# One decoder layer on one core: a later wait for the post-norm row, moved low parts and squares, and GpSimd making sums of weight blocks

## The chip, the cores and the metric

The kernel runs on one core of a Trainium2 chip. The metric is device time in microseconds of one execution, the median of several runs. The engines are called by the profile's names: PE (TensorE, matmuls), PEld (its weight loads), DVE (VectorE), ACT (ScalarE), POOL (GpSimd), SP (the queue that issues most transfers).

## The reference

One layer of a decoder on x of 256 x 2048, fp32, D_FF = 5504:

```
h = rmsnorm(x, g1);  x = x + 0.5 * rmsnorm((silu(h @ Wg) * (h @ Wu)) @ Wout, g1post)      # FFN 1
h = rmsnorm(x, g2);  proj = h @ w_in                       # q, k, v of two attentions, gates
y = (sigmoid(ga) * (diff_attn @ Wd) + sigmoid(gb) * (window_attn @ Ws)) @ w_out
x = x + rmsnorm(y, g2post)
h = rmsnorm(x, g3);  x = x + 0.5 * rmsnorm((silu(h @ Wg2) * (h @ Wu2)) @ Wout2, g3post)   # FFN 2
```

## The kernel before

**Split products.** Every fp32 operand is split into a rounded high part and a low part, the rest. A product of blocks is three matmuls of 128 x 128 by 128 x 512: high by high, high by low, low by high. Weights stream from memory. SP loads four blocks of 128 x 512 at a time into one of four `raw` buffers; half a buffer is a *sub*. For each sub ACT makes the high part (`w_hi`), DVE subtracts to get the low part (`w_lo`, one `tensor_tensor` with both inputs in SBUF), and PE then multiplies. ACT and DVE run three subs ahead (`LEAD = 3`); there are four places for split subs, so the split of sub s waits until PE has done sub s - 4. SP loads a buffer anew when DVE has made the low parts of its two subs.

**Gate and up products.** `gate_up` goes over 11 pairs of column chunks (the last one narrower), first the gate's chunk and then the up projection's. Pairs 1 to 8 save products with a scheme of sums of blocks. Below, the subs of a pair are numbered from 0 at the beginning of its gate. A standard sub takes 12 matmuls on PE, the others 6 or 3. In pairs 1 to 7 gate subs are standard but for 2 and 3 (cross, 6 each); of the up side 8 and 9 are standard, 10 and 11 are corner subs (3 each, one block wide), 12 and 13 the first *shared* product (6 each), 14 and 15 standard, 16 and 17 the second shared one (6 each), 18 and 19 standard. In pair 0 the subs 10 and 11 are standard. So there are two shared products in the up side of each of the pairs 0 to 7, in both FFNs: 32 in all. A shared product belongs to the next pair. Its buffer gets three blocks in two transfers (`three_blocks`, L397 and L399, the second telling `corner_in`). Before ACT splits it, DVE adds blocks in place in `block_sums`: one addition of 128 x 512 (L1206) and one of 128 x 1024 (L1207), each with two SBUF inputs. ACT waits for `sums_ready`.

**Beside them.** After each pair DVE transposes its activation in blocks (L1299), POOL moves the blocks through memory and back (`move_blocks`, L509 and L514, each with a wait), ACT makes the high part (`round_a`, L957) and DVE the low part (`rest_of_a`, L1306). ACT and DVE run these as hooks of the next pair's up side, both before the third sub that is split there (hook 2, before sub 13's split). In pair 0 ACT runs hooks while it splits the gate of the chunk: hook 6 makes the eight sums of squares of x (L941), which DVE (`pre_norm`, hook 7) makes a variance of, and POOL the root (L522), which the gate's activation (L989) needs.

**Down products.** `down` runs four output chunks of 24 subs each (8 in the mixer). ACT issues the transfer of the post-norm gain row (`gain`, broadcast to 128 partitions, 1 MB) when the last product before it is done, since it takes a place that holds operands of it. DVE waits for it before the first `steps` of `down`; the row is used in `take_y`, after the first chunk.

Every engine goes through its instructions in the order written; the order above is by hand.

## Time and profile before

| | us |
|---|---|
| median of 3 runs | 2040.34 |
| lowest, highest | 2038.36, 2040.49 |
| the profiled execution's own time | 2040.98 |
| its span, first to last instruction | 2039.2 |
| PE busy | 2008.6 |
| DVE busy | 1356.0 |
| ACT busy | 1046.5 |
| POOL busy | 87.0 |

Matmuls are pipelined: one lasts 0.39 us in the record while they start closer together than that, so a gap between records is shorter than the time lost. Times in a timeline are us from the span's start. A bracket at the end of a line is the engine's idle time before it and who ended it. A chain line has start, us and what.

### The profile page before, as it was taken

What the parts mean: (1) busy time and instruction counts of PE and PEld (TensorE: products, weight loads), DVE (VectorE), ACT (ScalarE), POOL (GpSimd) and SP (SyncE); (2) the same over time, 40 slices, a digit from 0 to 9 for tenths busy, and PEclk for the clock granted to TensorE, in tenths of its full rate; (3) what the DMA queues carried; (4) which work ended last, traced back from release to release, by engine and by line L of the source; (5) the groups of instructions that cost most, each with busy time, mean ns of one, the idle gap of its engine ahead of it and who ended that gap; (6) DMA issues with size and microseconds to landing.
All of it is one profiled execution on the core that took longest, in us unless ns stands there. A gap on an engine that the chain in (4) does not pass through costs nothing.

```text
span 2039.2 us, 23559 instructions
## 1 busy us (share of the span) xinstructions
PE 2008.6 (98%) x9154; PEld 1659.6 (81%) x9154; DVE 1356.0 (66%) x1514; ACT 1046.5 (51%) x1342; POOL 87.0 (4%) x144
## 2 busy tenths in 40 slices
PE   8999999999999999999999999999999999999997
PEld 6888888888888878888888888878888888978886
DVE  6888888756555574456655665588888886655554
ACT  6555555545444454446555544465555554544442
POOL 0000000001000000000100000000000000000000
PEclk9999999999999999999999999999999999999999
DMA  6777777767555655554444455456777777565553
GB/s 236 233 250 224 244 227 231 245 215 241 190 186 176 216 165 186 182 189 161 155 160 145 174 195 207 165 180 228 236 233 237 240 228 255 190 228 205 190 187 108
DMA packets 206440, 415.26 MB, mean 204 GB/s; under 512 B 9169, under 2 KB 17666, under 8 KB 205826
## 3 DMA queue, kind: packets, MB, share of 16 engines
q1 hardware_dynamic: 198610, 388.16, 56.8%
q0 software_dynamic: 7264, 22.55, 4.2%
q10 hardware_dynamic: 464, 3.15, 0.4%
q8 instruction: 69, 1.13, 0.2%
q14 instruction: 33, 0.27, 0.0%
HBM read 400.46 MB, written 13.37 MB: 203 GB/s over the span
## 4 chain that ended last, share of the span: by engine, by line
PE 95%; DVE 2%; DMA 1%; ACT 1%; issue 0%; POOL 0%; DVEq 0%; ACTq 0%; POOLq 0%
PE acc L552 17%; PE acc L554 17%; PE acc L553 17%; PE acc L629 11%; PE acc L630 11%; PE acc L631 11%; PE tp L629 3%; PE tp L630 3%; PE tp L631 3%; PE tp L579 1%; DMA gain<-in_ffn_norm_post 1%; PE tp L793 1%; PE tp L767 1%; DVE w_lo L1183 1%; PE tp L777 0%
## 5 line engine op out<-in xcount | busy, mean ns | idle before, releaser
L1183 DVE TENSOR_TENSOR w_lo<-raw,w_hi 128x1024 fp32r<-128x1024 f32 x408 | 497.1, 1225 | 457.6 <-ACT w_hi L880 441.1
L880 ACT ACTIVATE w_hi<-raw 128x1024 fp32r<-128x1024 f32 x408 | 429.0, 1058 | 444.2 <-PE acc L554 440.0
L902 ACT ACTIVATE w_hi<-raw 128x1024 fp32r<-128x1024 f32 (+1 forms) x400 | 405.0, 1024 | 331.9 <-PE acc L631 235.0
L1216 DVE TENSOR_TENSOR w_lo<-raw,w_hi 128x1024 fp32r<-128x1024 f32 (+1 forms) x400 | 465.7, 1179 | 146.8 <-ACT w_hi L902 143.5
L629 PE MATMUL acc<-w_hi,h_hi 128*128 128x512 f32 (+1 forms) x928 | 354.7, 382 | 0.8 <-DVE w_lo L1216 0.5
L631 PE MATMUL acc<-w_hi,h_lo 128*128 128x512 f32 (+1 forms) x928 | 354.1, 382 | 0.0
L630 PE MATMUL acc<-w_lo,h_hi 128*128 128x512 f32 (+1 forms) x928 | 354.0, 381 | 0.0
L552 PE MATMUL acc<-w_hi,h_hi 128*128 128x512 f32 x736 | 293.9, 399 | 8.8 <-DVE w_lo L1183 6.5
L554 PE MATMUL acc<-w_hi,h_lo 128*128 128x512 f32 x736 | 287.7, 391 | 0.0
L553 PE MATMUL acc<-w_lo,h_hi 128*128 128x512 f32 x736 | 287.0, 390 | 0.0
L552 PE MATMUL acc<-w_hi,a_hi 128*128 128x512 f32 x688 | 268.5, 390 | 4.9 <-DVE w_lo L1183 4.9
L553 PE MATMUL acc<-w_lo,a_hi 128*128 128x512 f32 x688 | 268.4, 390 | 0.0
L554 PE MATMUL acc<-w_hi,a_lo 128*128 128x512 f32 x688 | 268.4, 390 | 0.0
L629 PEld LDWEIGHTS acc<-w_hi,h_hi 128*128 128x128 f32 x928 | 174.2, 188 | 34.7 <-DVE w_lo L1216 2.4
L631 PEld LDWEIGHTS acc<-w_hi,h_lo 128*128 128x128 f32 x928 | 174.2, 188 | 31.2
L630 PEld LDWEIGHTS acc<-w_lo,h_hi 128*128 128x128 f32 x928 | 174.2, 188 | 30.9
L552 PEld LDWEIGHTS acc<-w_hi,h_hi 128*128 128x128 f32 x736 | 138.7, 188 | 39.3 <-issue 8.2
L554 PEld LDWEIGHTS acc<-w_hi,h_lo 128*128 128x128 f32 x736 | 138.5, 188 | 30.0
L553 PEld LDWEIGHTS acc<-w_lo,h_hi 128*128 128x128 f32 x736 | 138.9, 189 | 27.0
L552 PEld LDWEIGHTS acc<-w_hi,a_hi 128*128 128x128 f32 x688 | 129.6, 188 | 32.6 <-DVE w_lo L1183 5.7
L554 PEld LDWEIGHTS acc<-w_hi,a_lo 128*128 128x128 f32 x688 | 129.6, 188 | 27.0
L553 PEld LDWEIGHTS acc<-w_lo,a_hi 128*128 128x128 f32 x688 | 129.5, 188 | 26.8
(151 smaller groups left out, 1791.9 us busy)
## 6 DMA issues: line engine op xcount, KB each, us to landing
raw<-in_ffn_w_in SPq DMA_DIRECT2D x126, 1024.0 KB, 5.0
raw<-in_w_in SPq DMA_DIRECT2D x68, 1024.0 KB, 5.2
raw<-in_ffn_w_out SPq DMA_DIRECT2D x56, 1024.0 KB, 5.1
raw<-in_ffn_w_in SPq DMA_DIRECT2D x68, 512.0 KB, 4.4
raw<-in_ffn_w_out SPq DMA_DIRECT2D x40, 768.0 KB, 4.3
raw<-in_w_out SPq DMA_DIRECT2D x16, 1024.0 KB, 5.0
raw<-in_ffn_w_in SPq DMA_DIRECT2D x16, 768.0 KB, 4.4
bounce<-blocks POOLq DMA_DIRECT2D x20, 512.0 KB, 3.7
```

The lines of the kernel that those rows point to most:

```text
L552: nc.tensor.matmul(o, xh, wh, start=first, stop=False)
L553: nc.tensor.matmul(o, xh, wl, start=False, stop=False)
L554: mm = nc.tensor.matmul(o, xl, wh, start=False, stop=last)
L579: mm = nc.tensor.transpose(tp[:, b, t * P:(t + 1) * P], src(t), ident[:])
L629: nc.tensor.matmul(o[:, 0:width], x[0], wh, start=first, stop=False)
L630: nc.tensor.matmul(o[:, 0:width], x[0], wl, start=False, stop=False)
L631: return nc.tensor.matmul(o[:, 0:width], x[1], wh, start=False, stop=last)
L767: mm = nc.tensor.matmul(tp[:, 2 + c, m * P:P + 2 * m * P], qk[r, qt, m * P:(m + 1) * P], kt[:, 0:(m + 1) * P], start=True, stop=True)
L880: nc.scalar.activation(w_hi[:, s % 4], raw[:, g % 4, s % 2 * 2:s % 2 * 2 + 2], ACT.Copy)\
L902: nc.scalar.activation(w_hi[:, s % 4, 0:n], raw[:, g % 4, s % 2 * 2:s % 2 * 2 + n], ACT.Copy)\
L1183: nc.vector.tensor_tensor(w_lo[:, s % 4], raw[:, g % 4, s % 2 * 2:s % 2 * 2 + 2], w_hi[:, s % 4].bitcast(F32), ALU.subtract).then_inc(lo_r ...
L1216: nc.vector.tensor_tensor(w_lo[:, s % 4, 0:n], raw[:, g % 4, s % 2 * 2:s % 2 * 2 + n], w_hi[:, s % 4, 0:n].bitcast(F32), ALU.subtract).the ...
```

## The change

Three things change. In `down`, DVE's wait for the post-norm row stands behind the first output chunk's steps. In `gate_up`, the hook of `round_a` moves from 2 to 7 (5 where no shared product is in the up side) and that of `rest_of_a` from 2 to 8 (6); the eight squares are made in hooks 5, 6 and 7, three, three and two. And the shared products' two additions go from DVE to POOL, in the order of `move_blocks`: those of pair 0 before its first wait, those of pair i + 1 behind the landing of pair i's blocks. ACT waits for the new semaphore `shared_sums`; cross subs stay on DVE.

```diff
--- before.py
+++ after.py
@@ -84,7 +84,13 @@
 
 def sums_count(k, r):
 
-    made = [kind == CROSS or (kind == SHARED and half == 0) for kind, arg, half in FFN_SUBS]
+    made = [kind == CROSS for kind, arg, half in FFN_SUBS]
+    return k * sum(made) + sum(made[:r + 1])
+
+
+def shared_count(k, r):
+
+    made = [kind == SHARED and half == 0 for kind, arg, half in FFN_SUBS]
     return k * sum(made) + sum(made[:r + 1])
 
 
@@ -327,6 +333,8 @@
         dve_step = sem("dve_step")
         corner_in = [sem(f"corner_in{q}") for q in range(FAST)]
         sums_ready = sem("sums_ready")
+        shared_sums = sem("shared_sums")
+        corner_sum = sem("corner_sum")
         blocks_turned = sem("blocks_turned")
         blocks_out = sem("blocks_out")
         blocks_in = sem("blocks_in")
@@ -500,8 +508,23 @@
                                                          base=WINDOW - 1 - b, pattern=[[1, n]],
                                                          channel_multiplier=-1))
 
-            def move_blocks(k):
-
+            def block_sums(b8, k, i):
+
+                for arg in range(FAST):
+                    r = UP_AT[i] + 2 * pair_slots(i)[1].index((SHARED, arg))
+                    n = shared_count(k, r)
+                    g = (8 * b8 + r) // 2
+                    v = raw[:, g % 4]
+                    gp.wait_ge(raw_in[g % 4], 16 * (g // 4 + 1))
+                    gp.wait_ge(corner_in[arg], 16 * fast_count(k, i + 2))
+                    nc.gpsimd.tensor_tensor(v[:, 2, :], v[:, 2, :], v[:, 1, :], ALU.add).then_inc(corner_sum, 1)
+                    gp.wait_ge(corner_sum, n)
+                    nc.gpsimd.tensor_tensor(v[:, 1:4:2, :], v[:, 0:1, :].to_broadcast([P, 2, CW]), v[:, 1:3, :],
+                                            ALU.add).then_inc(shared_sums, 1)
+
+            def move_blocks(b8, k):
+
+                block_sums(b8, k, 0)
                 for i in range(PAIRS + 1):
                     n = (PAIRS + 1) * k + i + 1
                     width, held = (CW, bounce) if i < PAIRS else (TAIL, short_bounce)
@@ -513,6 +536,8 @@
                         dst = blocks[32 * b:32 * b + 32, 0:2 * width].rearrange("c (q x) -> c q x", q=4)
                         gp.dma_start(dst, rows_of[b]).then_inc(blocks_in, 16)
                     gp.wait_ge(blocks_in, 64 * n)
+                    if i + 2 in FAST_PAIRS:
+                        block_sums(b8, k, i + 1)
 
             for i, (n, m) in enumerate(ROOT_STEPS):
                 gp.wait_ge(var_ready, i + 1)
@@ -521,10 +546,10 @@
                 ms = slice(0, MT) if m is None else slice(m, m + 1)
                 nc.gpsimd.tensor_tensor(root[:, n, ms], var[:, n, ms], half[:, ms], ALU.pow).then_inc(root_ready, 1)
                 if n == R_PRE[0]:
-                    move_blocks(0)
+                    move_blocks(A8, 0)
                     distances()
                 elif n == R_PRE[2]:
-                    move_blocks(1)
+                    move_blocks(F8, 1)
 
 
         @block.tensor
@@ -893,8 +918,10 @@
                 kind, arg, half = kind_of(p + LEAD)
                 if s % 2 == 0:
                     act.wait_ge(raw_in[g % 4], 16 * (g // 4 + 1))
-                if kind in (CROSS, SHARED):
+                if kind == CROSS:
                     act.wait_ge(sums_ready, sums_count(k, p + LEAD))
+                elif kind == SHARED:
+                    act.wait_ge(shared_sums, shared_count(k, p + LEAD))
                 if kind == SHARED and half == 1:
                     nc.scalar.activation(t2[:, arg, :], raw[:, g % 4, 3, :], ACT.Copy)
                 act.wait_ge(multiplied, s - 3)
@@ -932,7 +959,8 @@
 
                 take = piece_parts(sc0)
                 return {1: lambda: take(2, 3), 2: lambda: take(4, 5),
-                        4: lambda: take(6, 7), 6: square_x(k)}
+                        4: lambda: take(6, 7),
+                        5: square_x(k, 0, 3), 6: square_x(k, 3, 6), 7: square_x(k, 6, MT * NG)}
 
             def square(n, src, total):
 
@@ -941,14 +969,14 @@
                 nc.scalar.activation(junk[:, 0:src.shape[-1]], src, ACT.Square, accum_out=total)\
                     .then_inc(squared, 1)
 
-            def square_x(k):
+            def square_x(k, first, last):
 
                 def hook():
-                    for m in range(MT):
-                        for q in range(NG):
-                            if k == 0:
-                                act.wait_ge(x_in[q], 16)
-                            square(Q_X[k] + m * NG + q, xs[:, m, q * CW:(q + 1) * CW], ssx[:, m, q:q + 1])
+                    for i in range(first, last):
+                        m, q = i // NG, i % NG
+                        if k == 0:
+                            act.wait_ge(x_in[q], 16)
+                        square(Q_X[k] + i, xs[:, m, q * CW:(q + 1) * CW], ssx[:, m, q:q + 1])
                 return hook
 
             def round_a(k, i):
@@ -971,7 +999,8 @@
                 for i in range(PAIRS + 1):
                     width = CW if i < PAIRS else TAIL
                     if i == 0:
-                        steps(b8, 8, {**hooks, 7: round_comb})
+                        last_squares = hooks[7]
+                        steps(b8, 8, {**hooks, 7: lambda: (round_comb(), last_squares())})
                         act.wait_ge(root_ready, root_count(R_PRE[k]))
                     else:
                         ffn_steps(b8, f, GATE_AT[i], UP_AT[i] - GATE_AT[i], {})
@@ -989,7 +1018,8 @@
                             nc.scalar.activation(stage[:, m, 0:width], acc[:, 0, m, 0:width], ACT.Silu,
                                                  scale=root[:, R_PRE[k], m:m + 1]).then_inc(acc_free[0], 1)
                     up = pair_slots(i)[1]
-                    before = {2: lambda: round_a(f, i - 1)} if i else {}
+                    late = 7 if (SHARED, FAST - 1) in up else 5
+                    before = {late: lambda: round_a(f, i - 1)} if i else {}
                     if (SHARED, FAST - 1) in up:
                         done = 2 * up.index((SHARED, FAST - 1)) + 2
                         before[done] = lambda: copy_shared(i, done)
@@ -1199,13 +1229,6 @@
                         dve.wait_ge(raw_in[g % 4], 16 * (g // 4 + 1))
                     nc.vector.tensor_tensor(v[:, 2 * half + 1, :], v[:, 2 * half, :], t2[:, half, :],
                                             ALU.add).then_inc(sums_ready, 1)
-                elif kind == SHARED and half == 0:
-                    uses = [i for i in FAST_PAIRS if UP_AT[i - 1] < r]
-                    dve.wait_ge(raw_in[g % 4], 16 * (g // 4 + 1))
-                    dve.wait_ge(corner_in[arg], 16 * (len(FAST_PAIRS) * k + len(uses)))
-                    link(nc.vector.tensor_tensor(v[:, 2, :], v[:, 2, :], v[:, 1, :], ALU.add))
-                    nc.vector.tensor_tensor(v[:, 1:4:2, :], v[:, 0:1, :].to_broadcast([P, 2, CW]), v[:, 1:3, :],
-                                            ALU.add).then_inc(sums_ready, 1)
 
             def ffn_split(b8, k, p):
                 s = 8 * b8 + p + LEAD
@@ -1367,7 +1390,8 @@
                                   fixes(i) if i in FAST_PAIRS else {})
                     before = {0: comb_rest} if i == 0 else {0: gate_out(i)} if i in FAST_PAIRS else {}
                     if i:
-                        before[2] = lambda: rest_of_a(f, i - 1)
+                        late = 8 if (SHARED, FAST - 1) in pair_slots(i)[1] else 6
+                        before[late] = lambda: rest_of_a(f, i - 1)
                     ffn_steps(b8, f, UP_AT[i], GATE_AT[i + 1] - UP_AT[i], before)
                     dve.wait_ge(multiplied, 8 * b8 + GATE_AT[i + 1])
                     if i in FAST_PAIRS:
@@ -1408,9 +1432,10 @@
                     link(nc.vector.tensor_reduce(ssum[:, m:m + 1], ssq[:, m, :], AX.X, ALU.add))
                     variance(R_POST[k], ssum[:, m:m + 1], D_MODEL, factor, slice(m, m + 1))
                 subs = 8 * units
-                dve.wait_ge(gain_in, 16 * (k + 1))
                 for n in range(NG - 1):
                     steps(b8 + n * units, subs, first if n == 0 else None)
+                    if n == 0:
+                        dve.wait_ge(gain_in, 16 * (k + 1))
                     for m in range(MT):
                         take_y(n, m)
                 update = residual(k)
```

## Rows read from the trace of the kernel before

**Rows 1.** The page's part 1: busy us (share of span), instructions.

```profile
PE 2008.6 (98%) x9154; PEld 1659.6 (81%) x9154; DVE 1356.0 (66%) x1514; ACT 1046.5 (51%) x1342; POOL 87.0 (4%) x144
```

**Rows 2.** List of waits: who waited for whom, us, times, longest.

```profile
DVE w_lo L1183 <- DMA gain<-in_ffn_norm_post: 11.3, 2, 5.7
...
PEld acc L629 <- DVE w_lo L1216: 8.3, 22, 0.7
...
PEld acc L629 <- DVE w_lo L1183: 1.1, 2, 0.6
```

**Rows 3.** Chain, then timeline (start, us, engine) at the first down stage.

```profile
477.70 7.92 DMA gain<-in_ffn_norm_post
...
485.64 5.77 DVE L1183 TENSOR_TENSOR w_lo<-raw,w_hi 128x1024 fp32r<-128x1024 f32 x5 [5.64 <-DMA gain<-in_ffn_norm_post]
...
486.92 0.50 PE L552 MATMUL acc<-w_hi,a_hi 128*128 128x512 f32 x1 [2.41 <-DVE w_lo L1183]
```

**Rows 4.** Timeline; window: length, busy PE, PEld, DVE, ACT, POOL, clock, DMA (second down).

```profile
1799.10 0.57 PE L552 MATMUL acc<-w_hi,a_hi 128*128 128x512 f32 x1 [2.48 <-DVE w_lo L1183]
...
1799.00:1802.40 3.40, 3.30 (x8) 2.63 (x9) 3.40 (x4) 0.56 (x1) 2.19 (x4) 0.56 0.58 151
```

**Rows 5.** Timeline of DVE, ACT and PE in a steady pair.

```profile
215.08 1.23 DVE L1207 TENSOR_TENSOR raw<-raw 128x1024 f32<-128x1024 f32 x1
216.22 0.69 DVE L1216 TENSOR_TENSOR w_lo<-raw,w_hi 128x512 fp32r<-128x512 f32 x1
...
218.62 1.29 DVE L1306 TENSOR_TENSOR a_lo<-blocks,a_hi 128x512 fp32r<-128x512 f32 x2
219.99 2.36 DVE L1216 TENSOR_TENSOR w_lo<-raw,w_hi 128x1024 fp32r<-128x1024 f32 x2
...
215.21 0.62 ACT L902 ACTIVATE w_hi<-raw 128x512 fp32r<-128x512 f32 x1
216.39 1.06 ACT L902 ACTIVATE w_hi<-raw 128x1024 fp32r<-128x1024 f32 x1 [0.56 <-DVE raw L1207]
...
219.76 0.39 PE L629 MATMUL acc<-w_hi,h_hi 128*128 128x512 f32 x1
...
220.89 0.39 PE L631 MATMUL tp<-w_hi,comb_lo 128*128 128x512 f32 x1
221.27 0.50 PE L629 MATMUL acc<-w_hi,comb_hi 128*128 128x512 f32 x1
```

**Rows 6.** One line's instructions: SP's transfer for the second shared product.

```profile
L399 SPq DMA_DIRECT2D raw<-in_ffn_w_in x1: 601/601/601, 210.7 to 210.7; - x1
...
DMA to landing us min/median/max: 4.3/4.3/4.3
```

**Rows 7.** POOL's groups by shape, and its line L522 (ns: least/median/most).

```profile
L496 POOL TENSOR_SCALAR_AFFINE_SELECT dist<-dist 128x256 f32<-128x256 f32 x2 | 0.8, 402 | 0.3
...
L482 POOL TENSOR_SCALAR_AFFINE_SELECT ident<-ident 128x128 f32<-128x128 f32 x1 | 0.3, 294 | 0.2 <-POOL ident L481 0.2
...
L522 POOL TENSOR_TENSOR root<-var,half x17: 544/1594/1607, 41.6 to 2029.3; 128x2 f32<-128x2 f32 x11, 128x1 f32<-128x1 f32 x6
```

**Rows 8.** Timeline of DVE and POOL where both work.

```profile
500.64 2.53 DVE L1183 TENSOR_TENSOR w_lo<-raw,w_hi 128x1024 fp32r<-128x1024 f32 x2 [0.78 <-ACT w_hi L880]
...
502.17 1.16 POOL L499 TENSOR_SCALAR_AFFINE_SELECT dist<-dist 128x128 f32<-128x128 f32 x1
```

**Rows 9.** Timeline of PE, DVE and ACT in pair 0.

```profile
41.26 0.50 PE L629 MATMUL acc<-w_hi,h_hi 128*128 128x512 f32 x1 [0.19 <-DVE w_lo L1183]
...
47.22 0.50 PE L629 MATMUL acc<-w_hi,h_hi 128*128 128x512 f32 x1 [0.23 <-DVE w_lo L1216]
...
41.31 0.17 DVE L1270 TENSOR_SCALAR var<-ssum 128x2 f32<-128x2 f32 x1
...
42.95 1.22 DVE L1330 TENSOR_TENSOR comb_lo<-comb,comb_hi 128x1024 fp32r<-128x1024 f32 x1
...
44.24 1.06 ACT L902 ACTIVATE w_hi<-raw 128x1024 fp32r<-128x1024 f32 x1
```

## The prediction

> **What bounds the kernel now.** I began with the page's busy times: TensorE (PE) is busy for 98% of the span [rows 1]. Work taken from another engine is worth nothing by itself; only PE's idle time, some 30 us, can be won or made larger. The list of waits says who ends PE's idle stretches: always a low part that VectorE (DVE) makes. Two kinds bear on the change. Twice DVE stood 5.7 us behind the post-norm row's transfer, and 22 + 2 times PE's weight load waited up to 0.7 us for a low part inside the gate and up products [rows 2]. The timeline prices the first kind [rows 3, 4], and one steady pair (the fourth after pair 0) and pair 0 the second [rows 5, 9].
>
> **The post-norm row's wait.** In `down`, DVE waits for the row before its first low part. The row takes 7.9 us from its issue at 477.70, DVE resumes at 485.64 and PE restarts at 486.92 after 2.41 us without work [rows 3]. Matmuls start 0.23 us apart and last 0.39 [rows 5], so 0.16 us of overlap is lost too, and the restarted one takes 0.50, which is 0.11 more: 2.7 us. In the second FFN it is 2.48 + 0.16 = 2.64 us, and then the granted clock reads 0.56 for 3.4 us: eight matmuls fill 3.30 us where at 0.23 they want 1.8, so 1.5 us more [rows 4]. Sum 6.8 us. The new place is behind 24 subs of the first output chunk (about 60 us; 8 subs, about 22 us, in the mixer's), so the 7.9 us are hidden. Next in line would be DVE's own work: its low part follows the two transposes of the last pair, and three subs are already split ahead, so PE has 6.8 us of work when `down` begins. I leave nothing exposed: **-6.8 us**. The mixer's instance is not among the waits of PE, and I count it as 0.
>
> **Low parts of activations and squares, moved.** In pairs 1 to 7, PE's sub 13 (second shared one) starts at 221.27, though the last matmul of sub 12 started at 220.89 and the next was due at 221.12. So 0.15 us is lost, and with the slow restart (0.50) 0.26 us [rows 5]. It waited for DVE's low part, which stood behind the 1.29 us of `rest_of_a` at 218.62 [rows 5], while ScalarE (ACT) made the high one behind `round_a`. Both now come five or more subs later, where subs last 2.7 us. There the pipeline of two splits (1.06 and 1.23 us) leaves over 3 us, which hides their 1.3 and 1.1 us, so moving them costs 0. Alone it would take away 14 x 0.26 = 3.7 us. The squares move from before sub 9's split to three places; in pair 0 PE waits for sub 9 (0.19 idle + 0.16 + 0.11 = 0.46 us) and for sub 11 (0.23 + 0.16 + 0.11 = 0.50) [rows 9]. The first vanishes: the high part of sub 9 comes two squares (1.6 us) earlier. Part of it returns at sub 11, whose high part comes from ACT at 44.24 to 45.30, behind the tenth sub's split, the table load and the gate's activation [rows 9], so PE could have it at about 46.9 when it now wants it at 46.35.
>
> **The sums on GpSimd (POOL).** Taken from DVE: 32 x (0.69 + 1.23) us, the long one as at 215.08, the short one as wide as the low part at 216.22 [rows 5]. Given to POOL: 64 additions. Their price is not in the trace. One input and one output: 294 ns at 128 columns, 402 at 256, or 0.84 ns per column and 0.19 us fixed [rows 7]. Below: 0.62 us for 512 columns, 1.05 for 1024. Above: three such streams (two read, one written) and the fixed part of POOL's own two-input form, at most 0.54 [rows 7]: 1.8 and 3.1 us. I take the middle, 1.2 and 2.1.
>
> Behind POOL's new waits (transfers landed, first addition done) stands only the next move of the blocks, due at the pair's end some 20 us later: 0. ACT's new wait on them is for a sum made well before the second shared sub's high part is wanted at about 222.5 us.
>
> Does it hide? DVE's low parts read two tensors of SBUF, as POOL's additions do. At 502.17 a POOL select of 128 columns, 0.29 us alone, takes 1.16 us and ends 0.16 us after DVE's low part ends at 503.17 [rows 7, 8]; POOL's two-input roots have a median of 1.59 us against a least of 0.54 [rows 7]. So POOL is held while such a DVE instruction runs. That DVE is held while POOL reads, no row shows: POOL reads nothing long here. The bounds are none and the whole instruction; I take the whole, since what keeps one of them out should keep out the other.
>
> The Trainium skill says the same for both directions (SBUF — State Buffer, Who interferes with whom): the pair of ports is an exclusive lock, and a DVE instruction with two SBUF inputs contends with a GpSimd one that reads SBUF. The trace agrees for POOL; no run here shows it yet for DVE. With the price of its GPSIMD Engine Reference, Performance versus the Vector engine (4497 ns for 2048 columns, so an estimate of 2.3 us for 1024), the sum below would be some 4 us higher.
>
> **A steady pair with DVE held.** The first shared sub's blocks land long before its use, and DVE has time there. The second's second transfer is issued at 210.7 and takes 4.3 us [rows 6]: 215.0. POOL adds 512 columns from 215.0 to 216.2. DVE could begin the half-width low part of sub 11 at 215.8 (its high part: 215.21 + 0.62), is held to 216.2, then runs to 216.9. POOL's 1024-column addition waits for that and reads until 218.9 (2.1 less the 0.16 of rows 7 and 8). Sub 12's high part needs only sub 8 now, so it ends near 216.9 instead of 217.45; its low part would start then, but is held to 218.9 and ends at 220.1. PE wants it at 219.76: 0.35 + 0.11 = 0.46 us. After it, sub 13 (high part 219.5) is in time. So the place of the wait moves one sub forward, and 0.26 becomes 0.46: 14 x 0.20 = **+2.8 us**. The point from which it decides: no stall if the long addition takes under 1.75 us.
>
> **Pair 0 with DVE held.** POOL is behind the root (var at 41.3, root until 42.3) and starts the sums when DVE is busiest. In turns: sub 10's low part to 43.35, short addition to 44.4, `comb_lo` to 45.6, long addition to 47.6, sub 11's low part to 48.8, where PE wants it at 46.35: 2.5 us + 0.11. The second shared sums, already landed, follow at once: short one to 49.9, low part of 12 to 51.1, long one to 53.1, low part of 13 to 54.3, wanted at 53.05: 1.3 + 0.11. Together 4.0 us, for 0.96 now: +3.1, and twice (the second FFN's pair 0 has the same order): **+6.2 us**.
>
> **Sum.** -6.8 + 2.8 + 6.2 = +2.2 on the profiled execution's 2040.98 us, or 2043.2. That execution lies 0.64 above the median of the runs, 2040.34, so the forecast is 2042.5 us: the profitable edit is paid away by the lock.
>
> **The rivals.**
> 1. *DVE is not held.* Only POOL waits. Speaks for it: no DVE instruction in the trace is lengthened by POOL. Against: the same resource holds POOL. Then -6.8 - 3.7, and in pair 0 0.61 instead of 0.96, twice: -11.2, or 2029 us.
> 2. *DVE is held, but the additions are cheap* (long one under 1.75 us, down to 1.05). Steady pairs lose their stall, pair 0 stays about as it is: -6.8 - 3.7 = -10.5, or 2030 us; at 1.75 still some -6.
> 3. *The other side: the long addition takes 2.5 us or more.* At 2.8 us DVE's low part of sub 12 comes 0.7 us later again in each steady pair, +12.6 instead of +2.8, and pair 0 gives 4.5 instead of 3.1: -6.8 + 12.6 + 9 = +14.8, or 2055 us. From 2.2 us on, the sum is slower by more than can be measured.
> 4. *The row's wait turns into another at the same place.* The trace speaks against it: ACT's splits ran ahead of DVE at 478 to 484. If it did, 1 to 2 us of the 6.8 stay.
>
> **Chances.** The forecast's case (DVE held, long addition 1.75 to 2.5 us) 0.58; DVE not held 0.22; cheap additions 0.12; dear ones 0.08. The measurement tells 0.2% (4 us). The forecast's case gives by its price 2036 to 2050, and I split it 0.04 faster, 0.32 same, 0.22 slower. Faster: 0.04 + 0.22 + 0.12 = 0.38; same 0.32; slower 0.22 + 0.08 = 0.30. The range takes in the rivals on the fast side and stops short of rival 3: 2028.5 to 2050. The likeliest case alone has 2036 to 2050.
>
> **What would show it.** PE's waits of 2.4 us at the start of both `down` stages gone, and the clock at 1.00 there. The column of POOL's TENSOR_TENSOR of 1024 columns: its least duration is the price. DVE's `w_lo` beside it: starts late or lasts over 1.23 us if held. The steady pair's stall should be before sub 12, not 13, at about 0.46 us; a stall of over 2 us before sub 11 of pair 0. If PE has no wait at all in steady pairs, rival 1 or 2 is right, and `w_lo`'s durations tell which. I am wrong most easily in the assumption that DVE is held, and in POOL's price, where 0.1 us is worth about 2 us of the total.

## The result: 0.5% slower, and the profile after

| | before, us | changed, us |
|---|---|---|
| median of 5 runs | 2040.34 | 2050.69 |
| lowest, highest | 2038.36, 2040.89 | 2048.11, 2052.95 |
| profiled execution, its span | 2040.98, 2039.2 | 2050.81, 2049.0 |

The ratio is 1.0050, with an interval from 1.0036 to 1.0064: slower, clear of the noise, but by well under 2%. The forecast was 2042.5 us with a range to 2050.0; the measured time lies just above the range.

Where the time went is told by the lengths of the stages, each from the start of its first matmul in the trace to the start of the next stage's first:

| stage, us | before | changed | difference |
|---|---|---|---|
| gate and up, first FFN | 467.4 | 474.9 | +7.5 |
| down, first FFN | 239.0 | 238.2 | -0.8 |
| mixer | 607.2 | 606.8 | -0.4 |
| gate and up, second FFN | 465.9 | 473.0 | +7.1 |
| down, second FFN, to the end | 249.6 | 245.7 | -3.9 |

These make +9.5 us; the spans differ by 9.8, of which 0.2 lies ahead of the first of these matmuls. First the page of the changed kernel, part 1 (busy us, share, instructions), which answers to [rows 1]:

```profile
PE 2007.4 (98%) x9154; PEld 1662.2 (81%) x9154; DVE 1349.8 (66%) x1450; ACT 1048.1 (51%) x1342; POOL 230.5 (11%) x208
```

POOL has 143 us more, yet DVE only 6 us less: 64 additions of 0.69 and 1.23 us, 61 us in all, left DVE, and most of what they freed came back as longer instructions. That is the first sign that the two hold each other. The list of waits (us, times, longest) answers to [rows 2]:

```profile
PE acc L654 <- DVE w_lo L1239: 15.1, 17, 1.8
...
PEld acc L654 <- DVE w_lo L1239: 10.5, 6, 2.2
ACT a_hi L985 <- DMA blocks<-short_bounce: 9.6, 2, 5.4
```

The row's wait is gone from the list. In its place PE waits 17 + 6 times for a low part in the gate and up products, now up to 2.2 us where it was 0.7, and ACT waits twice, up to 5.4 us, for the last pair's blocks. Three windows of the changed kernel: the beginning of each `down`, and a stretch in pair 0 of the second FFN. Columns: length, busy PE, PEld, DVE, ACT, POOL, granted clock, share and rate of DMA. They answer to [rows 4]:

```profile
485.00:500.00 15.00, 15.00 (x68) 12.45 (x67) 11.15 (x12) 7.45 (x7) 2.74 (x5) 1.00 0.94 321
1799.00:1806.00 7.00, 7.00 (x38) 6.51 (x37) 6.40 (x10) 3.19 (x3) 0.00 (x0) 1.00 0.73 226
1367.00:1370.40 3.40, 3.40 (x10) 2.72 (x11) 3.40 (x2) 2.36 (x3) 3.32 (x2) 0.61 0.66 198
```

At the head of both `down` stages PE is busy all the time with the clock at 1.00, as expected. But in the second FFN the low clock (full speed is 2.4 GHz, the lower level 1.2) has moved: after PE's stall of 1.79 us in pair 0 (its restart at 1366.94) the granted clock reads 0.61 on the mean of the window from 1367.0 to 1370.4. From 1368 to 1371 matmuls start 0.43 us apart instead of 0.23, which is the lower level.

**A steady pair.** The timeline of the changed kernel (start, us, engine) in two steady pairs of the first FFN, in each POOL's sums for the second shared product, DVE's low parts and PE's restart. They answer to [rows 5]:

```profile
177.02 1.29 POOL L520 TENSOR_TENSOR raw<-raw 128x512 f32<-128x512 f32 x1 [0.94 <-DMA raw<-in_ffn_w_in]
178.40 2.73 POOL L522 TENSOR_TENSOR raw<-raw 128x1024 f32<-128x1024 f32 x1
...
177.83 1.04 DVE L1239 TENSOR_TENSOR w_lo<-raw,w_hi 128x512 fp32r<-128x512 f32 x1 [1.41 <-ACT w_hi L929]
179.03 8.86 DVE L1239 TENSOR_TENSOR w_lo<-raw,w_hi 128x1024 fp32r<-128x1024 f32 x6 [0.16 <-ACT w_hi L929]
...
181.51 0.39 PE L656 MATMUL tp<-w_hi,comb_lo 128*128 128x512 f32 x1
182.36 0.47 PE L654 MATMUL acc<-w_hi,h_hi 128*128 128x512 f32 x1 [0.46 <-DVE w_lo L1239]
...
221.70 1.29 POOL L520 TENSOR_TENSOR raw<-raw 128x512 f32<-128x512 f32 x1 [1.86 <-DMA raw<-in_ffn_w_in]
223.07 3.26 POOL L522 TENSOR_TENSOR raw<-raw 128x1024 f32<-128x1024 f32 x1
...
221.90 2.17 DVE L1239 TENSOR_TENSOR w_lo<-raw,w_hi 128x1024 fp32r<-128x1024 f32 x1 [0.51 <-ACT w_hi L929]
224.54 5.14 DVE L1239 TENSOR_TENSOR w_lo<-raw,w_hi 128x1024 fp32r<-128x1024 f32 x3 [0.47 <-ACT w_hi L929]
...
225.74 0.39 PE L656 MATMUL tp<-w_hi,comb_lo 128*128 128x512 f32 x1
227.47 0.50 PE L654 MATMUL acc<-w_hi,comb_hi 128*128 128x512 f32 x1 [1.34 <-DVE w_lo L1239]
```

In the first of the two the course is the forecast's: the half-width low part of sub 11 is held to 178.87, sub 12's (the first of the group at 179.03: six take 8.86 us, while two unheld ones take 2.36 [rows 5], so six some 7.1) comes late, and PE stands before sub 12. The last matmul of sub 11 began at 181.51, the next was due at 181.74 and starts at 182.36: 0.62 + 0.11 for the slow restart = 0.73 us. In the second the low part of sub 12 takes 2.17 us, and the next one, begun at 224.54, is the first of three that take 5.14 us (3.5 at the same rate), because POOL's long addition runs from 223.07 to 226.33. PE stands before sub 13 instead, due at 225.97 and started at 227.47: 1.61 us. The line of SP's second transfer for the second shared product in the same two pairs tells them apart; it answers to [rows 6]:

```profile
L407 SPq DMA_DIRECT2D raw<-in_ffn_w_in x1: 601/601/601, 172.6 to 172.6; - x1
...
DMA to landing us min/median/max: 4.3/4.3/4.3
...
L407 SPq DMA_DIRECT2D raw<-in_ffn_w_in x1: 601/601/601, 215.5 to 215.5; - x1
...
DMA to landing us min/median/max: 6.1/6.1/6.1
```

The transfer issued at 172.6 took 4.3 us as before, the one issued at 215.5 took 6.1. So POOL began 1.8 us later there, and its hold fell on the low part after the one that I had walked through.

POOL's two lines and DVE's low parts (ns least/median/most), which answer to [rows 7]; before, L1216 had 1.23 us as its longest:

```profile
L520 POOL TENSOR_TENSOR raw<-raw x32: 1282/1297/2360, 41.8 to 1668.0; 128x512 f32<-128x512 f32 x32
...
L522 POOL TENSOR_TENSOR raw<-raw x32: 2720/2847/3279, 44.1 to 1669.3; 128x1024 f32<-128x1024 f32 x32
...
L1239 DVE TENSOR_TENSOR w_lo<-raw,w_hi x400: 691/1225/3425, 45.2 to 1802.5; 128x1024 fp32r<-128x1024 f32 x123, 128x512 fp32r<-128x512 f32 x11
```

**Pair 0** of the changed kernel, POOL, DVE and PE, in answer to [rows 9]:

```profile
41.83 2.19 POOL L520 TENSOR_TENSOR raw<-raw 128x512 f32<-128x512 f32 x1
44.10 3.24 POOL L522 TENSOR_TENSOR raw<-raw 128x1024 f32<-128x1024 f32 x1
...
42.78 2.32 DVE L1353 TENSOR_TENSOR comb_lo<-comb,comb_hi 128x1024 fp32r<-128x1024 f32 x1
45.17 11.10 DVE L1239 TENSOR_TENSOR w_lo<-raw,w_hi 128x1024 fp32r<-128x1024 f32 x5
...
46.39 0.39 PE L656 MATMUL acc<-w_hi,h_lo 128*128 128x512 f32 x1
48.48 0.50 PE L654 MATMUL acc<-w_hi,h_hi 128*128 128x512 f32 x1 [1.71 <-DVE w_lo L1239]
```

`comb_lo`, 1.22 us alone, takes 2.32; the short addition, 1.28 alone, takes 2.19. PE's sub 11 was due at 46.62 and starts at 48.48: 1.86 + 0.11 = 1.97 us. A second one of 1.47 us follows before sub 13.

### The profile page after: what moved, and what is told of

Its sections match the earlier page's. It is cut to its first block, busy times and chain, and to the rows that moved or that the text cites. A ratio compares the mean times of both kernels' runs of the same rounds, so it can differ in the third digit from the quotient of the medians.

```text
span 2049.0 us, 23545 instructions
## 1 busy us (share of the span) xinstructions
PE 2007.4 (98%) x9154; PEld 1662.2 (81%) x9154; DVE 1349.8 (66%) x1450; ACT 1048.1 (51%) x1342; POOL 230.5 (11%) x208
## 4 chain that ended last, share of the span: by engine, by line
PE 89%; DVE 4%; issue 4%; ACT 1%; DMA 1%; POOL 0%; DVEq 0%; ACTq 0%; POOLq 0%
PE acc L577 16%; PE acc L579 16%; PE acc L578 16%; PE acc L654 10%; PE acc L655 10%; PE acc L656 10%; DVE w_lo L1239 3%; PE tp L656 3%; PE tp L655 3%; PE tp L654 3%; ACT w_hi L929 1%; PE tp L818 1%; PE tp L604 1%; PE tp L792 1%; PE tp L802 0%
## 5 line engine op out<-in xcount | busy, mean ns | idle before, releaser
L1239 DVE TENSOR_TENSOR w_lo<-raw,w_hi 128x1024 fp32r<-128x1024 f32 (+1 forms) x400 | 512.7, 1305 | 174.9 <-ACT w_hi L929 172.8
```

Source lines behind the costliest of these rows:

```text
L1239: nc.vector.tensor_tensor(w_lo[:, s % 4, 0:n], raw[:, g % 4, s % 2 * 2:s % 2 * 2 + n], w_hi[:, s % 4, 0:n].bitcast(F32), ALU.subtract).the ...
```

## Experiments

Times are medians with the number of runs; the ratio is to the kernel before on the same chip (2040.66, 2040.17 or 2040.29 us). "The base" is the kernel before with the row's wait, the low parts and the squares moved, and the sums left on DVE; it is the third of the kernels below.

### The parts one by one

Only the row's wait moved:

```diff
-                dve.wait_ge(gain_in, 16 * (k + 1))
                 for n in range(NG - 1):
                     steps(b8 + n * units, subs, first if n == 0 else None)
+                    if n == 0:
+                        dve.wait_ge(gain_in, 16 * (k + 1))
```

> The kernel before with one edit: the wait for the post-norm row behind the first output chunk. Theory A (the prediction's step): both stalls at the start of the down stages go and nothing takes their place, -6.8 us, 2033.5. Theory B (from the changed kernel's trace, where PE stood 1.8 us in the first down stage in front of a low part behind the last pair's blocks): a second wait takes over in the first FFN, for the blocks that POOL moves through memory, so some -4.6 us (0.8 + 3.8), 2035.7.

Only the low parts of activations and the squares moved (the squares as in the change):

```diff
-                    before = {2: lambda: round_a(f, i - 1)} if i else {}
+                    late = 7 if (SHARED, FAST - 1) in up else 5
+                    before = {late: lambda: round_a(f, i - 1)} if i else {}
...
-                        before[2] = lambda: rest_of_a(f, i - 1)
+                        late = 8 if (SHARED, FAST - 1) in pair_slots(i)[1] else 6
+                        before[late] = lambda: rest_of_a(f, i - 1)
```

> The kernel before with the moved low parts and squares alone; sums stay on VectorE. The prediction's step: -3.7 us for 14 steady pairs and up to -0.9 for the first stall of each pair 0, some of which returns: 2035.7 to 2036.6. Rival: the sums on VectorE, which come in the same steps, keep the stall where it is and the move gives under 1 us.

Both of them, the base:

> The changed kernel with the sums of blocks given back to VectorE. If the sums on GpSimd are the whole loss, this is 2030 to 2032 us, 19 to 21 us under the changed kernel. If a part of the loss comes from the moves (a high part that ScalarE makes late), it is 2036 or more.

Only the sums on POOL, the rest as before:

> The kernel before with the sums on GpSimd alone: the hooks and the row's wait as before. If VectorE is held by GpSimd: slower by 15 to 20 us (what the changed kernel shows in both gate and up stages, 7.7 + 7.1 us, and 3.7 us that the moves gave back, as the stall of sub 13 now has the low part of the activations in front of it too), 2055 to 2060. If the hold matters only together with the moves: under 2048.

| | median, us | ratio, interval | against before |
|---|---|---|---|
| row's wait | 2035.52 (11) | 0.9979, 0.9970 to 0.9988 | -5.1 |
| low parts and squares | 2035.03 (11) | 0.9973, 0.9964 to 0.9982 | -5.6 |
| both, the base | 2030.47 (5) | 0.9953, 0.9939 to 0.9967 | -10.2 |
| sums on POOL | 2069.48 (4) | 1.0143, 1.0128 to 1.0159 | +28.8 |

The first three came within 1 us of what was expected (theory B for the row's wait); the sums alone cost 9 us more than the 2055 to 2060 expected. The two moves add up (-5.1 - 5.6 = -10.7, for -10.2 measured together). The sums on POOL cost 28.8 us alone and 2050.69 - 2030.47 = 20.2 us on the base. So the whole loss is theirs, and the moves take away 8.6 us of it. The likely reason, which no run sets apart, is that the low parts of activations no longer stand in the same queue. By stage the moves give -2.4 us in gate and up of the first FFN, -2.3 in the second, and -0.9 in the mixer, which I had not counted.

With the row's wait moved, `down` of the first FFN is 2.0 us shorter and that of the second 2.9; the list of waits (us, times, longest) of that kernel has the reason:

```profile
ACT a_hi L957 <- DMA blocks<-short_bounce: 9.2, 2, 5.0
```

### Who holds whom

On the base, POOL does additions of 512 and of 1024 columns at the same two points of every pair 0 to 7, but on a scratch place that nobody reads or waits for; DVE makes the real sums.

```diff
+                    nc.gpsimd.tensor_tensor(spare_sum[:, 0:CW], spare_sum[:, 0:CW], spare_sum[:, CW:2 * CW], ALU.add).then_inc(corner_sum, 1)
+                    gp.wait_ge(corner_sum, corner_steps[0])
...
+                    nc.gpsimd.tensor_tensor(spare_sum[:, 0:2 * CW], spare_sum[:, 0:2 * CW], spare_sum[:, 0:2 * CW], ALU.add).then_inc(corner_sum, 1)
+                    gp.wait_ge(corner_sum, corner_steps[0])
```

> The changed kernel's wait and moves, the sums on VectorE; GpSimd makes, at the same points, additions of 512 and 1024 columns on a place of its own that nobody waits for (each input is read as in the sums). If the cost is that VectorE is held while GpSimd reads: slower than without them (2030.5) by about what the changed kernel pays, 15 to 25 us, and the low parts of 1.23 us last up to 3.4. If the cost is that the sums are late on GpSimd: 2030 to 2032, since nobody waits for them.

And the same with four `memset` of 1024 columns in place of the two additions, which write but read nothing (one of the four is shown):

```diff
-                    nc.gpsimd.tensor_tensor(spare_sum[:, 0:CW], spare_sum[:, 0:CW], spare_sum[:, CW:2 * CW], ALU.add).then_inc(corner_sum, 1)
+                    nc.gpsimd.memset(spare_sum[:, 0:2 * CW], 0.0).then_inc(corner_sum, 1)
```

> As the run before, but in place of the two additions four fills of 1024 columns, which read nothing and together last about as long (4 us against 3.6). If only reading holds VectorE: 2030 to 2032 and no low part over 1.3 us. If any work of GpSimd on SBUF holds it: 2045 or more.

Measured: reading 2065.20 us (4 runs; 1.0124, 1.0107 to 1.0141), writing 2029.40 (4; 0.9949, 0.9932 to 0.9965), against 2030.47 of the base. The line of DVE's low parts with reading additions (ns least/median/most), and PE's wait for it:

```profile
L1241 DVE TENSOR_TENSOR w_lo<-raw,w_hi x400: 691/1224/2914, 48.4 to 1816.2; 128x1024 fp32r<-128x1024 f32 x123, 128x512 fp32r<-128x512 f32 x11
...
PE acc L651 <- DVE w_lo L1241: 26.3, 16, 4.1
```

And one place in that kernel's timeline, in a steady pair: POOL's addition, DVE's low parts (four, one of them of half width, which unheld would take some 4.2 us: 3 x 1.18 + 0.69), PE's restart:

```profile
183.32 2.22 POOL L518 TENSOR_TENSOR spare_sum<-spare_sum 128x1024 f32<-128x1024 f32 x1
...
182.00 6.89 DVE L1241 TENSOR_TENSOR w_lo<-raw,w_hi 128x512 fp32r<-128x512 f32 x4
...
186.77 0.47 PE L651 MATMUL acc<-w_hi,h_hi 128*128 128x512 f32 x1 [1.07 <-DVE w_lo L1241]
```

The writing kernel, POOL's group (us, mean ns) and DVE's low parts:

```profile
L524 POOL MEMSET spare_sum<- 128x1024 f32 x32 | 30.6, 956 | 1.8
...
L1246 DVE TENSOR_TENSOR w_lo<-raw,w_hi x400: 683/1224/1228, 45.8 to 1781.2; 128x1024 fp32r<-128x1024 f32 x123, 128x512 fp32r<-128x512 f32 x11
```

Nobody waits for these instructions in either kernel, and POOL is busy with them for about the same time in both (127 and 122 us). Additions cost 35 us and stretch DVE's longest low part from 1.23 to 2.9 us; memsets cost nothing and leave it at 1.228. So POOL holds DVE when it reads and not when it only writes, and rival 1 falls. The 35 us are above the 15 to 25 expected. Set matmul by matmul beside the base (every kernel here issues the same 9154 matmuls in the same order), the reading kernel loses 21.8 us in the fourteen pairs 1 to 7 and 11.9 in the two pairs 0, where PE stands for 4.0 and 4.1 us and the granted clock is at its lower level for 6.8 us around each restart. This answers what the prediction left open of the Trainium skill (SBUF — State Buffer, Who interferes with whom): a DVE instruction with two SBUF inputs contends with a GpSimd one that reads and not with one that only writes. The runs agree in both directions.

### In small pieces

The changed kernel with each addition cut into pieces that write 128 columns (four and eight instructions in place of one and one; a piece of the long sum takes 64 columns of each of its two output blocks). The edit of the short sum:

```diff
-                    nc.gpsimd.tensor_tensor(v[:, 2, :], v[:, 2, :], v[:, 1, :], ALU.add).then_inc(corner_sum, 1)
+                    for c in range(4):
+                        x = slice(c * P, (c + 1) * P)
+                        ins = nc.gpsimd.tensor_tensor(v[:, 2, x], v[:, 2, x], v[:, 1, x], ALU.add)
+                    ins.then_inc(corner_sum, 1)
```

> The changed kernel with each sum in pieces of 128 columns (four and eight instructions instead of one and one). If VectorE is held for one GpSimd instruction at a time and gets its turn behind it, a hold lasts some 0.3 us and not 2.2: most of the 20 us come back, 2034 to 2040, though GpSimd takes longer. If it is held until GpSimd's queue is empty: 2050 or more.

Measured: 2049.22 us (4 runs; 1.0045, 1.0028 to 1.0061), no gain over the changed kernel that could be told, where 2034 to 2040 was expected. The line of the long sums' pieces, who waited for it (us, times), then POOL, DVE and PE in pair 0:

```profile
L527 POOL TENSOR_TENSOR raw<-raw x256: 450/462/1502, 45.4 to 1676.1; 128x128 f32<-128x128 f32 x128
...
  ACT w_hi L935: 56.1, 16
...
45.35 4.25 POOL L527 TENSOR_TENSOR raw<-raw 128x128 f32<-128x128 f32 x8
...
45.01 1.35 DVE L1245 TENSOR_TENSOR w_lo<-raw,w_hi 128x1024 fp32r<-128x1024 f32 x1 [0.90 <-ACT w_hi L935]
50.77 4.36 DVE L1245 TENSOR_TENSOR w_lo<-raw,w_hi 128x1024 fp32r<-128x1024 f32 x3 [4.42 <-ACT w_hi L935]
...
52.48 0.77 PE L660 MATMUL acc<-w_hi,h_hi 128*128 128x512 f32 x1 [3.06 <-DVE w_lo L1245]
```

DVE is no longer held for long: the low part at 45.01 lasts 1.35 us, and the longest of the 400 lasts 1.57. But a piece costs at least 0.45 us, eight of them 4.25, and a piece waits in its turn for DVE (1.5 us at most). Now it is ACT that waits for POOL's sums, 56 us in 16 times, and PE stands for 3.06 us before 52.48. Set beside the base in the same way, the fourteen pairs 1 to 7 lose 9.9 us where the changed kernel loses 13.3, so the pieces do help there. The two pairs 0 lose 8.9 where it loses 5.9, since PE stands for 3.06 us in each. In the first FFN the granted clock is at its lower level for 6.8 us around that restart (it reads 0.50 from 52 to 58) and pair 0 loses 5.6 us; in the second it stays at 1.00 and pair 0 loses 3.3. So part of the gain was lost to lateness in pair 0, and some 2.3 us of that to the clock.

### Which of the two products

The changed kernel with only the first shared product's sums on POOL and the second's on DVE (`range(FAST)` becomes `range(1)` in POOL's `block_sums`, the counts follow):

> The changed kernel with the second shared product's sums given back to VectorE; the first's stay on GpSimd. By the walk through a steady pair, the first's additions fall where VectorE has time, so steady pairs cost next to nothing and what is left is pair 0 at sub 11: +3 to +5 on 2030.5, 2033 to 2036. Rival: both shared products cost alike, 2040.

And the reverse, only the second's on POOL:

```diff
-                for arg in range(FAST):
+                for arg in range(1, FAST):
```

> The changed kernel with the first shared product's sums given back to VectorE; the second's stay on GpSimd. If the hold in front of subs 12 and 13 is the loss: 10 to 16 us over the kernel without GpSimd's sums (2030.5), 2041 to 2046, where the first's alone cost 3.7. If the two share the loss only when both are there: under 2038.

Measured: first alone 2034.19 us (6 runs; 0.9969, 0.9956 to 0.9981), +3.7 over the base; second alone 2063.04 (4; 1.0112, 1.0096 to 1.0128), +32.6; both, as in the change, +20.2. With the first alone, POOL's long addition (ns least/median/most) and pair 0's restart:

```profile
L522 POOL TENSOR_TENSOR raw<-raw x16: 2402/2848/3258, 43.6 to 1645.7; 128x1024 f32<-128x1024 f32 x16
...
48.00 0.50 PE L654 MATMUL acc<-w_hi,h_hi 128*128 128x512 f32 x1 [1.71 <-DVE w_lo L1246]
```

Its steady pairs have no wait of PE. Gate and up are 1.0 and 1.3 us longer than the base's, for pair 0, and `down` of the second FFN 2.3, where PE stands 2.04 us behind the last pair's blocks (the wait of the next section); `down` of the first is 1.2 shorter. So the +3.7 falls into the expected range, but a third of it comes from `down` and not from pair 0. In this kernel lies also the clean price of the long addition: 2.40 us. Only one of the 16 shows it, the one at 213.0, which has no DVE instruction with two SBUF inputs beside it; the others wait for a low part.

With the second alone, DVE, POOL and PE in the steady pair that is also shown above:

```profile
224.49 0.69 DVE L1236 TENSOR_TENSOR raw<-raw 128x512 f32<-128x512 f32 x1
225.21 1.23 DVE L1237 TENSOR_TENSOR raw<-raw 128x1024 f32<-128x1024 f32 x1
226.35 6.25 DVE L1246 TENSOR_TENSOR w_lo<-raw,w_hi 128x512 fp32r<-128x512 f32 x3
...
225.36 2.22 POOL L520 TENSOR_TENSOR raw<-raw 128x512 f32<-128x512 f32 x1 [11.27 <-DMA raw<-in_ffn_w_in]
227.66 2.73 POOL L522 TENSOR_TENSOR raw<-raw 128x1024 f32<-128x1024 f32 x1
...
231.62 0.47 PE L654 MATMUL acc<-w_hi,h_hi 128*128 128x512 f32 x1 [1.57 <-DVE w_lo L1246]
```

The second alone was expected at 2041 to 2046 and missed that by 17 us. Against the base it loses 24.5 us in the fourteen pairs 1 to 7, where the change loses 13.3, and 7.6 in the two pairs 0 (5.9). The timeline shows how in this pair. DVE now makes the first product's sums itself, from 224.49 to 226.44, and these read two inputs too. POOL's short addition begins beside the long one of them and takes 2.22 us instead of 1.28, so the long one starts only at 227.66 and lies on the low parts that PE wants next: it stands 1.57 us before 231.62. In the changed kernel the first product's sums are long done on POOL by then.

### The wait behind the row's wait

The base, with the last pair's blocks (the last piece of the activation) split at hooks 14 and 15 of `down` instead of 7 and 8, in both FFNs:

```diff
-            down(B8, 3, 0, ffn1_norm_post, SC_BC, {7: lambda: round_a(0, PAIRS)})
+            down(B8, 3, 0, ffn1_norm_post, SC_BC, {14: lambda: round_a(0, PAIRS)})
...
-            down(B8, 3, 0, 0.5, {8: lambda: rest_of_a(0, PAIRS)})
+            down(B8, 3, 0, 0.5, {15: lambda: rest_of_a(0, PAIRS)})
```

> The wait behind the first output chunk, the moves, the sums on VectorE, and the last pair's blocks taken in at subs 14 and 15 of the first output chunk instead of 7 and 8. If the blocks' way through memory is the wait that took the row's place (1.14 us in front of PE in the first FFN, and the restart), this is 1.2 to 1.5 us under the same kernel without the last edit (2030.5): 2029. If something else is next, no change.

And the same hooks in the kernel that has only the row's wait moved:

> The kernel before with the row's wait moved and the last pair's blocks taken in at subs 14 and 15. The prediction's 6.8 us should appear whole when no second wait follows: 2033.5; against 2035.5 with the row's wait alone.

Measured: 2028.43 us (5 runs, 2028.21 to 2028.68; 0.9942, 0.9928 to 0.9957), and 2033.82 (6; 0.9970, 0.9957 to 0.9982). Against before, the second has `down` shorter by 2.7 and 4.4 us, where the row's wait moved alone gave 2.0 and 2.9. PE's waits for low parts in the first of the two kernels (us, times, longest):

```profile
PEld acc L629 <- DVE w_lo L1219: 1.5, 2, 0.8
...
PE acc L629 <- DVE w_lo L1219: 0.6, 2, 0.4
```

These 1.5 + 0.6 us are all that is left in the gate and up products, and the first `down` has no idle time of PE in the timeline, where the base still had 0.97 us before 496.89. The gain of 2.0 us over the base is somewhat more than the 1.2 to 1.5 expected. This version is the fastest found: 12 us faster than before, and by the medians 22 us faster than the changed kernel.

## Why the prediction was wrong, step by step

1. **Row's wait (-6.8).** Right in mechanism: both stalls and the low clock behind the second are gone. Too large in size: -0.8 and -3.9 us in the changed kernel's two `down` stages, -4.7. Rival 4, which I had at 1 to 2 us, is partly true, in another form. ACT's high part of the last pair's blocks waits for POOL's transfer chain, which the row's wait had hidden. The timeline of the changed kernel, ACT, DVE and PE in the first `down`, in the place of [rows 3]:

```profile
504.22 0.94 ACT L985 ACTIVATE a_hi<-blocks 128x384 fp32r<-128x384 f32 x2 [5.43 <-DMA blocks<-short_bounce]
...
506.14 1.22 DVE L1213 TENSOR_TENSOR w_lo<-raw,w_hi 128x1024 fp32r<-128x1024 f32 x1 [6.09 <-ACT w_hi L905]
...
505.46 0.39 PE L579 MATMUL acc<-w_hi,a_lo 128*128 128x512 f32 x1
507.42 0.51 PE L577 MATMUL acc<-w_hi,a_hi 128*128 128x512 f32 x1 [1.57 <-DVE w_lo L1213]
```

ACT stands 5.43 us until 504.22, its splits follow, DVE has none to make a low part of for 6.09 us, and PE, due at 505.69, starts at 507.42: 1.73 + 0.11 = 1.84 us lost. In the second FFN the same place costs 0.44 + 0.11. I had looked at three subs split ahead at the start of `down` and not at the hooks behind them. That this is the cause is shown: with the blocks at hooks 14 and 15 the kernel with the row's wait moved gains 1.7 us more (2035.52 to 2033.82), and the base 2.0. Then the whole is -6.5 (2040.29 to 2033.82), which is the forecast's term.

2. **Moved low parts and squares (0 beside the sums, -3.7 and up to -0.9 alone).** Confirmed, a little small: -5.6 measured, of which 0.9 in the mixer.

3. **DVE is held by POOL's reads (taken as the whole instruction, 0.58 with this price).** Right, shown by the reading and the writing kernel; rivals 1 (2029 us) and 2 (2030) had their sums right: without a hold of DVE the kernel takes 2029.40 (POOL only writes) or 2030.47 us (the base).

4. **A steady pair (+2.8): the step that failed.** The fourteen stalls of the changed kernel, from start to start with the slow restart, are 1.75, 0.69, 0.73, 1.61, 0.76, 1.19, 0.66 us in the first FFN and 1.06, 0.85, 1.29, 0.99, 0.80, 1.08, 0.76 in the second: 14.2 us for 3.7 before, or +10.5. Set matmul by matmul beside the kernel before, these pairs are 9.4 us longer; most of the rest is that a restart before sub 12 takes 0.47 us and not 0.50, and so loses less than the 0.11 counted. Two things were mis-sized.

   The price: "I take the middle, 1.2 and 2.1" for additions that take 1.28 and 2.40. With the long one 0.30 longer, the same walk gives 0.76 us a stall in place of 0.46, and seven of the fourteen are 0.66 to 0.85. That is 14 x 0.30 = 4.2 us.

   The time at which the second product's blocks are there: the other seven stalls sum to 8.97, or 3.7 more than 7 x 0.76. I had taken 4.3 us from one pair [rows 6] as the landing time of all. The trace of the changed kernel has 4.3, 4.2, 4.3, 6.1, 4.3, 5.5, 4.2 us in the first FFN and 4.1, 4.4, 5.7, 4.5, 4.3, 4.6, 4.3 in the second. Those of 4.4 to 4.6 go with stalls of 0.85 to 1.08. The three of 5.5 to 6.1 go with stalls of 1.19 to 1.61, before sub 13; the other eleven stalls are before sub 12. Pair 1 of each FFN (1.75 and 1.06) has a usual landing time, but the transfer is issued 8.1 and 8.6 us before sub 12 is due, where all the others have 9.1: there the short addition of the first product holds the low part (2.22 us in the first FFN, 1.71 in the second) that SP waits for before it loads the buffer anew. So with both products on POOL the first one's sums are not free in pair 1. The kernel before has 4.1 to 5.1 us for the same fourteen transfers. Why three of them land later here stays open, and no run sets the landing apart from the price.

The estimate with the price of the Trainium skill (GPSIMD Engine Reference, Performance versus the Vector engine), 2.3 us for 1024 columns, was nearer to the 2.40 measured than my 2.1. The sum made with it, some 4 us higher, would have been about 2046.5 us.

5. **Pair 0 (+6.2).** About right in the sum: 1.97 + 1.47 us in the first FFN for 0.96 before; in the second 2.06 and about 1.6 for the low clock, for 0.91: +5.2. In the second FFN that is in part luck, since the stall forecast before sub 13 did not come and the low clock, which I had not forecast, took its place. The turns came in the order that I had walked through, but about 0.5 us earlier, as the low part of sub 10 ended at 42.87 and not at 43.35. A record of a held instruction includes its wait: the short addition ends at 44.02 and `comb_lo` at 45.10, where I had 44.4 and 45.6. So the dearer additions made it no worse than forecast.

6. **The sum.** -4.7 + 9.4 + 5.2 - 0.4 in the mixer = +9.5, which is what the stages make. The misses of steps 1 and 4, 2.1 and 6.6 us, go the same way. Of the rivals, rival 3 (2.5 us or more, 2055 us) is nearest: the clean price lies between its case and mine. The sign that I had named, the least duration in the changed kernel, is 2.72 and would say rival 3, but 0.3 of it is a wait for a low part. And "from 2.2 us on, slower by more than can be measured" held. The range ended at 2050 because I bounded it by my own case and gave a price of over 2.5 us only 0.08, though the upper bound from the rows was 3.1.

## What to carry to other kernels

Before moving two-input work from VectorE to GpSimd, ask what VectorE does in that time and not how busy GpSimd is: here 61 us of work taken away cost 20 to 29 us, because the reading additions of pair 0 and of the second product hold a low part that TensorE wants next, and a longer price or a later landing moves the hold. Cutting the work small traded the hold for lateness in pair 0; a place where VectorE has nothing urgent (the first shared product in steady pairs) cost nothing when it was moved alone. When a wait is taken away, look for what it hid in the hooks behind it, and move that as well.

## What the hardware showed that was not expected

- The hold is per instruction and in both directions. Beside each other, a low part of 1.23 us took up to 3.43, a 512-column addition of 1.28 us up to 2.36, and the 1024-column one of 2.40 up to 3.28. With POOL's work in pieces of 0.45 us the longest low part took 1.57.
- In the one place where it can be seen, an input in PSUM took part in no hold: the 1024-column addition at 213.0 took its 2.40 us beside two DVE additions of `gate_fix` and the accumulator `acc`, which is in PSUM, and these took 0.69 and 0.68 us as in the kernel before.
- POOL's fp32 addition of two inputs took at least 450 ns for 128 columns, 1282 for 512 and 2402 for 1024: 2.17 ns a column and 0.17 us fixed. A one-input select took 0.84 ns a column [rows 7]; as it is another operation, what the second input costs by itself is not shown. A memset of 1024 columns took 956 ns and held nobody.
- More of the same work on POOL can be cheaper than less: +20.2 us for both products, +32.6 for the second alone.
- After a stall the granted clock was sometimes low and sometimes not. In the changed kernel it was at its lower level for 3.4 us behind 1.79 us of idle in pair 0 of the second FFN, while the kernel with the first product's sums alone on POOL has the same 1.79 us in the same place and full clock. In the kernel with small pieces PE stood 3.06 us in both pairs 0: the clock was low for 6.8 us in the first FFN and full in the second.
